# A list scheduler orders each engine's queue in the dense stages, barriers inside them go, and the scan constants are built in two halves

## The chip, the cores and the metric

The kernel runs on all 8 cores of one Trainium2 chip; each core works alone on 2048 of the 16384 tokens and nothing is exchanged. The metric is the device time of the slowest core in microseconds, lower is better. Times of several runs are given by their median; the trace is of one profiled execution on its slowest core, core 7.

## The reference

One decoder layer on `x` (4, 4096, 1024), cut to what matters:

```python
hn = rmsnorm(x, norm1); proj = hn @ w_in            # 1024 -> u, v, s, 512 each
o_a = gmlp(u, v)         # gelu, rmsnorm, causal 128x128 mix per head, product
bu = einsum(b_bar, s)    # S5: 32 groups, 64 complex states each
states = scan(a_bar, bu) # x_t = a * x_{t-1} + bu_t along the whole sequence
y = gelu(real(C @ states) + d_skip * s)
gl = y @ w_glu + b_glu;  o_b = gl[:, :512] * sigmoid(gl[:, 512:])
h = x + concat(rmsnorm(o_a), rmsnorm(o_b)) @ w_out
h = h + hier_moe(rmsnorm(h))      # top-1 of 4 groups, top-2 of 8 experts
h = h + sigmoid(rmsnorm(h) @ w_ple_gate) * (p @ w_ple_proj)
out = rmsnorm(h)
```

A core that holds the second half of a sequence needs the scan's state at its start. It gets it by running the scan's input part over the 2048 tokens before its own (`xprev`, the halo input); cores with a first half do the same work on zeros.

## The kernel before

A small recorder class `Prog` collects every instruction with its engine and its dependencies, and `emit` writes them out: each engine gets its instructions **in the order in which the program text recorded them**, with a semaphore wait where a dependency crosses engines, and also within an engine except on TensorE. `barrier()` (line 176) makes every engine wait for the last instruction of all engines and all open DMAs. `pipeline(nt, stages)` records a loop over tiles in software-pipelined order, the latest stage of the oldest tile first.

The stages, by their place in the text:

- **Setup** (lines 459 to 633): loads of small parameters and of `Wins`, then a chain of VectorE operations on [128, 16] that computes the discretised scan constants, their powers (`pwr`, `Rr`, `Ri`), the big products `PNr/PNi`, `QNr/QNi`, `QMr/QMi` of 2048 columns by `cmul` (six operations each), the copies masked by `hmask` into `QTp` and `QMp`, then on TensorE the matrices `MT` and `PT`. A barrier ends it.
- **A**, the S5 half, in four blocks of 1024 tokens, 0 and 1 from `xprev`, 2 and 3 from `x`. `A_front` loads 8 tiles, normalises (ACT square and copy, rstd on POOL by `rstd_from_ss`), transposes on TensorE, multiplies by `Wins` and transposes again into `Ub2[blk % 2]`. `A_level1` makes the scan input on TensorE into PSUM `psA`/`psB` and scans it on VectorE: 2 halves of 2 segments per block, each segment 4 multiplies out of PSUM, 2 adds, 16 scans, 6 small operations and, for blocks 2 and 3, four more large products of which POOL does two. `A_out(blk, 0)` multiplies by `QTp` and `MT` and applies gelu; `A_out(blk, 1)` transposes, runs the GLU as an 8-step pipeline and transposes into `mixTb`. Order in the text: front 0, front 1, level1 0, front 2, level1 1, front 3, level1 2, level1 3 first half, out(2,0), level1 3 second half, out(2,1), out(3,0), out(3,1). A barrier (line 833) ends it, and only then are the weights `Winu`, `Winv`, `Wout` and the inputs of B loaded.
- **B** (to line 947), the gMLP half and the output projection, 16 tiles of 128 tokens in a pipeline of 10 stages, its result `hd` stored to DRAM. In every second tile POOL issues the load of one expert's weights into the ring (`wload`, 7 of them). A barrier.
- **N** (to line 1016), norm and router logits, 16 tiles, 3 more `wload`; a barrier. **Routing**, one chain of VectorE operations, to the barrier in line 1122.
- **Experts** (to line 1293), gathers, three products and scatters for 32 experts. **C**, the last stage, 16 tiles in a pipeline of 8 stages, to line 1375.

## Time and profile before

| | us |
|---|---|
| median of 3 runs (1679.38 to 1686.72) | 1685.34 |
| the profiled execution, own time | 1668.8 |
| its span, core 7 | 1667.2 |
| spans of the eight cores | 1645.4 to 1667.2 |
| PE busy | 796.6 (48%) |
| DVE (VectorE) busy | 777.6 (47%) |
| ACT (ScalarE) busy | 577.4 (35%) |
| POOL (GpSimd) busy | 375.5 (23%) |

No engine is busy for half of the span. The page's 40 slices show that this is not even over time: DVE leads alone in the first slices and again from 380 to 500 us, PE in stage B. So the reading goes stage by stage, with the busy times of each stretch between two barriers.

### The profile page before, as it was taken

What the parts mean: (1) busy time and instruction counts of PE and PEld (TensorE: products, weight loads), DVE (VectorE), ACT (ScalarE), POOL (GpSimd) and SP (SyncE); (2) the same over time, 40 slices, a digit from 0 to 9 for tenths busy, and PEclk for the clock granted to TensorE, in tenths of its full rate; (3) what the DMA queues carried; (4) which work ended last, traced back from release to release, by engine and by line L of the source; (5) the groups of instructions that cost most, each with busy time, mean ns of one, the idle gap of its engine ahead of it and who ended that gap; (6) DMA issues with size and microseconds to landing.
All of it is one profiled execution on the core that took longest, in us unless ns stands there. A gap on an engine that the chain in (4) does not pass through costs nothing.

```text
span 1667.2 us, 20718 instructions; the slowest of 8 cores (1645.4 to 1667.2 us)
## 1 busy us (share of the span) xinstructions
PE 796.6 (48%) x5539; PEld 509.2 (31%) x5539; DVE 777.6 (47%) x1454; ACT 577.4 (35%) x831; POOL 375.5 (23%) x500
## 2 busy tenths in 40 slices
PE   0041553450244505777644525667555655807663
PEld 0040332330223202333213414455434443503231
DVE  5960226638874403444315673444233432325773
ACT  0004536540025543322204501554324443314543
POOL 0001101102322111322101105333223242202433
PEclk9995775775567856988875557887777877757887
DMA  2005313100000047566568502895557689165651
GB/s 42 0 0 138 90 53 99 63 15 0 1 1 1 0 83 156 159 183 165 151 181 209 165 7 100 301 297 204 181 204 269 224 273 248 45 212 174 235 197 76
DMA packets 68985, 216.76 MB, mean 130 GB/s; under 512 B 16585, under 2 KB 23753, under 8 KB 60368
## 3 DMA queue, kind: packets, MB, share of 16 engines
q1 hardware_dynamic: 42688, 164.97, 29.1%
q0 software_dynamic: 26128, 49.86, 13.4%
q8 instruction: 66, 1.08, 0.3%
q14 instruction: 103, 0.84, 0.2%
HBM read 212.14 MB, written 58.72 MB: 162 GB/s over the span
## 4 chain that ended last, share of the span: by engine, by line
PE 32%; DMA 21%; DVE 17%; issue 15%; ACT 8%; POOL 4%; SPq 1%; DVEq 1%; POOLq 1%; ACTq 0%; PEldq 0%
PE p L360 26%; DVE t L327 8%; DMA yd<-t,t 7%; ACT t L351 5%; PE p L364 5%; DVE t L337 5%; DMA t<-xnd,t 4%; DMA t<-x 3%; POOL t L327 3%; DMA t<-hd 3%; ACT t L355 2%; DVE t L357 2%; DMA t<-w_pg 2%; DVE t L333 1%; DMA t<-xprev 1%
## 5 line engine op out<-in xcount | busy, mean ns | idle before, releaser
L360 PE MATMUL p<-t,t 128*128 128x512 bf16 (+7 forms) x3811 | 636.0, 337 | 322.9 <-DVE t L333 140.5
L360 PEld LDWEIGHTS p<-t,t 128*128 128x128 bf16 (+2 forms) x3811 | 369.7, 121 | 556.2 <-issue 425.1
L364 PE MATMUL p<-t,t 128*128 128x128 bf16 (+1 forms) x1728 | 177.7, 270 | 526.6 <-DVE t L337 185.8
L364 PEld LDWEIGHTS p<-t,t 128*128 128x128 bf16 (+1 forms) x1728 | 142.6, 122 | 580.3 <-issue 575.5
L351 ACT ACTIVATE t<-t 128x1024 bf16<-128x1024 f32 (+4 forms) x172 | 150.8, 878 | 323.5 <-DVE t L327 133.6
L327 DVE TENSOR_TENSOR t<-t,p 128x512 f32<-128x512 f32 (+2 forms) x148 | 105.5, 742 | 330.3 <-PE p L360 258.2
L327 DVE TENSOR_TENSOR t<-t,t 128x512 f32<-128x512 f32 (+10 forms) x343 | 180.2, 547 | 96.7 <-DMA t<-maskS 43.1
L337 DVE SCALAR_TENSOR_TENSOR t<-t,t,t 128x1024 f32<-128x1024 f32 (+2 forms) x144 | 169.2, 1190 | 86.0 <-POOL t L327 61.2
L327 POOL TENSOR_TENSOR t<-t,t 128x1 f32<-128x1 f32 (+3 forms) x184 | 170.0, 928 | 153.6 <-DVE t L327 131.8
L357 DVE COPY t<-p 128x1024 bf16<-128x1024 bf16 (+1 forms) x182 | 122.3, 687 | 166.7 <-DMA yd<-t,t 92.6
L355 ACT COPY t<-p 128x512 f32<-128x512 f32 (+3 forms) x162 | 141.3, 911 | 163.9 <-DMA yd<-t,t 99.9
L333 POOL TENSOR_SCALAR t<-t 128x1 f32<-128x1 f32 x144 | 30.1, 209 | 633.3 <-ACT t L351 599.6
L390 POOL DMA_INDIRECT yd<-t,t x72 | 76.7, 1065 | 201.1 <-DVE t L357 77.2
L355 ACT CAST t<-t 128x1024 bf16<-128x1024 f32 (+2 forms) x100 | 91.8, 930 | 85.4 <-DVE t L337 64.1
L351 ACT ACT_TABLE_LOAD x17 | 21.8, 1283 | 259.2 <-DVE t L327 158.5
L384 POOL DMA_INDIRECT t<-xnd,t x72 | 75.4, 1048 | 62.6 <-DMA t<-xnd,t 35.8
L351 ACT ACTIVATE t<-p 128x512 f32<-128x512 f32 (+1 forms) x100 | 56.9, 590 | 51.4 <-PE p L360 48.8
L327 DVE TENSOR_TENSOR t<-p,t 128x512 f32<-128x512 f32 (+2 forms) x89 | 51.0, 595 | 46.6 <-PE p L360 37.7
L368 DVE TENSOR_TENSOR_SCAN t<-t,t,t 128x64 f32<-128x64 f32 x256 | 63.9, 325 | 0.6 <-DVE t L368 0.6
L357 DVE CAST t<-t 128x1024 bf16<-128x1024 f32 (+3 forms) x77 | 47.8, 625 | 28.7 <-DMA t<-wall 16.2
L355 ACT CAST t<-p 128x512 bf16<-128x512 f32 x28 | 16.0, 587 | 116.2 <-PE p L364 78.8
L351 ACT ACTIVATE t<-t,t 128x1024 bf16<-128x1024 f32 x32 | 36.8, 1150 | 39.6 <-POOL t L327 39.6
(33 smaller groups left out, 181.0 us busy)
## 6 DMA issues: line engine op xcount, KB each, us to landing
t<-wall SPq DMA_DIRECT2D x66, 1024.0 KB, 8.7
t<-x SPq DMA_DIRECT2D x48, 512.0 KB, 4.4
t<-hd SPq DMA_DIRECT2D x32, 512.0 KB, 5.7
t<-yd SPq DMA_DIRECT2D x32, 512.0 KB, 5.7
t<-wall POOLq DMA_DIRECT2D x10, 1536.0 KB, 12.7
t<-xprev SPq DMA_DIRECT2D x16, 512.0 KB, 3.6
hd<-t SPq DMA_DIRECT2D x16, 512.0 KB, 3.2
out<-t SPq DMA_DIRECT2D x16, 512.0 KB, 3.0
```

Of the source, the lines that this page charges most:

```text
L327: self.add(eng, lambda e: e.tensor_tensor(out=out.ap, in0=a.ap, in1=b.ap, op=op), **self._rw(out, (a, b), pw))
L333: self.add(eng, lambda e: e.tensor_scalar(out=out.ap, in0=a.ap, scalar1=self._a(s1), scalar2=self._a(s2), op0=op0, **kw), **self._rw(out, ...
L337: self.add("dve", lambda e: e.scalar_tensor_tensor(out=out.ap, in0=a.ap, scalar=self._a(s), in1=b.ap, op0=op0, op1=op1), **self._rw(out, ( ...
L351: self.add("act", lambda e: e.activation(out=out.ap, in_=a.ap, func=func, **kw), **rw)
L355: self.add("act", lambda e: e.copy(out=out.ap, in_=a.ap), **self._rw(out, (a,), pw))
L357: self.add(eng, lambda e: e.tensor_copy(out=out.ap, in_=a.ap), **self._rw(out, (a,), pw))
L360: self.add("pe", lambda e: e.matmul(out.ap, lhsT=lhsT.ap, rhs=rhs.ap, start=start, stop=stop), reads=list(lhsT.keys) + list(rhs.keys), pwr ...
L364: self.add("pe", lambda e: e.transpose(out=out.ap, in_=a.ap, identity=ident.ap), reads=list(a.keys) + list(ident.keys), pwrites=list(out.k ...
L368: self.add("dve", lambda e: e.tensor_tensor_scan(out=out.ap, data0=d0.ap, data1=d1.ap, initial=self._a(init), op0=ALU.mult, op1=ALU.add), ...
L384: self.add("pool", lambda e: e.indirect_dma_start(out=out.ap, out_offset=None, in_=table.ap, in_offset=bass.IndirectOffsetOnAxis(ap=idx.ap ...
L390: self.add("pool", lambda e: e.indirect_dma_start(out=table.ap, out_offset=bass.IndirectOffsetOnAxis(ap=idx.ap, axis=0), in_=a.ap, in_offs ...
```

## The change

- Every instruction gets an estimated cost and every SBUF and PSUM tile its address range. A tile that is put over older ones takes over their instructions as predecessors (`claim`), so memory is handed on without a barrier.
- The barriers in lines 632, 633, 833, 947 and 1016 are dropped. Those in front of the experts, behind them and at the end stay. They cut the program into segments 0 (setup, A, B, N, routing), 1 (experts) and 2 (C).
- `arrange` orders segments 0 and 2: it goes through the instructions in modelled time and gives each engine, whenever it is free, the ready instruction with the longest remaining chain. A group of accumulating matmuls stays together. The engines still run their queues strictly in that order. The expert stage keeps its order.
- Scratch tiles of the setup are put behind the tiles of the front (`Ub2`, `Zb2`, `xT_blk`, `xst`, `xnb`), so that a front can run beside the setup. `T1`, `T2`, `TA`, `Xr2`, `Xi2` and others of A lie over that scratch.
- The constants are built in two halves of 8 group pairs. The mask goes: `QT` holds both groups of a pair in the two halves of the partitions, and the matmuls read 64 partitions. ACT writes `QT`, and the minus sign of `QM` is made in `cmul`.
- `d_skip` and the B-half gain get their own tile `dg_bc`, the gains of the norms one tile per stage at the same address. The one-hot tiles of the routing have four buffers for two.

```diff
+    def claim(self, key, lo, hi):
+        t = len(self.tiles)
+        inherit = set()
+        for old in self.tiles:
+            if old["lo"] < hi and lo < old["hi"]:
+                inherit |= old["ops"]
+                old["live"] = False
+        self.tiles.append({"lo": lo, "hi": hi, "ops": set(), "inherit": inherit, "live": True, "key": key})
+        assert key not in KEYT, key
+        KEYT[key] = t
+        return t
...
+            if k in KEYT:
+                s["war"] = list(self.tiles[KEYT[k]]["inherit"])
...
+        for k in tuple(reads) + tuple(writes) + tuple(pwrites):
+            if k in KEYT:
+                tl = self.tiles[KEYT[k]]
+                assert tl["live"], k
+                tl["ops"].add(op.idx)
...
+    def arrange(self, ops):
+
+        own = {op.idx: op for op in ops}
+        units = {}
+        for op in ops:
+            units.setdefault((op.eng, op.grp), []).append(op)
+        uid = {}
+        ulist = []
+        for u in units.values():
+            for op in u:
+                uid[op.idx] = len(ulist)
+            ulist.append(u)
+        nu = len(ulist)
+        preds = [set() for _ in range(nu)]
+        succs = [set() for _ in range(nu)]
+        for op in ops:
+            for d in op.deps:
+                if d in own and uid[d] != uid[op.idx]:
+                    preds[uid[op.idx]].add(uid[d])
+                    succs[uid[d]].add(uid[op.idx])
+        cost = [sum(op.cost for op in u) for u in ulist]
+        eng = [u[0].eng for u in ulist]
+        dma = [u[0].is_dma for u in ulist]
+        full = [cost[i] + (2000 + ulist[i][0].size // 250 if dma[i] else 0) for i in range(nu)]
+        order = sorted(range(nu), key=lambda i: ulist[i][0].idx)
+        tail = [0] * nu
+        left = [len(x) for x in succs]
+        stack = [i for i in range(nu) if left[i] == 0]
+        while stack:
+            i = stack.pop()
+            tail[i] = full[i] + max([tail[j] + (60 if eng[j] == eng[i] else 180) for j in succs[i]], default=0)
+            for p in preds[i]:
+                left[p] -= 1
+                if left[p] == 0:
+                    stack.append(p)
+        wait = [len(x) for x in preds]
+        est = [0] * nu
+        avail = {}
+        for i in order:
+            if wait[i] == 0:
+                avail.setdefault(eng[i], []).append(i)
+        free = {}
+        dma_free = 0
+        out = []
+        done = 0
+        while done < nu:
+            best = None
+            for e, lst in avail.items():
+                if not lst:
+                    continue
+                f = free.get(e, 0)
+                t = max(f, min(est[i] for i in lst))
+                if best is None or t < best[0]:
+                    best = (t, e)
+            t, e = best
+            lst = avail[e]
+            pick = max((i for i in lst if est[i] <= t + 40), key=lambda i: (tail[i], -ulist[i][0].idx))
+            lst.remove(pick)
+            start = max(t, est[pick])
+            free[e] = start + cost[pick]
+            end = free[e]
+            if dma[pick]:
+                sz = ulist[pick][0].size
+                b = max(end, dma_free)
+                dma_free = b + sz // 300
+                end = dma_free + 2000
+            out.append((start, done, pick))
+            done += 1
+            for j in succs[pick]:
+                lag = 0 if eng[j] == "pe" and e == "pe" else (60 if eng[j] == e and not dma[pick] else 180)
+                est[j] = max(est[j], end + lag)
+                wait[j] -= 1
+                if wait[j] == 0:
+                    avail.setdefault(eng[j], []).append(j)
+        streams = {}
+        for _, _, i in out:
+            streams.setdefault(eng[i], []).extend(ulist[i])
+        return streams
...
+        for seg in range(self.seg + 1):
+            part = [op for op in ops if op.seg == seg]
+            got = {e: [op for op in part if op.eng == e] for e in engs}
+            if seg in self.sched:
+                head = [op for op in part if op.fn is None]
+                got = self.arrange([op for op in part if op.fn is not None])
+                for e in engs:
+                    got[e] = got.get(e, []) + [op for op in head if op.eng == e]
+            for e in engs:
+                streams[e].extend(got[e])
...
+    def _c(eng, n, k):
+        if eng == "dve":
+            return int(65 + max(110, k * n))
+        if eng == "act":
+            return int(210 + 0.83 * n)
+        return int(150 + 2.0 * n) if n > 1 else 450
...
+        self.add(q, lambda e: e.dma_start(out=oap, in_=iap, **kw), reads=rd, is_dma=True, cls=cls, size=size, cost=(1000 if q == "pool" else 400), **which)
...
+                 reads=list(lhsT.keys) + list(rhs.keys), pwrites=list(out.keys), grp=self.mmg, cost=30 + int(0.42 * _n(rhs)))
...
+    P.sched = {0, 2}
...
-    es_a = Mem(HLO, TOP - 16384)
+    es_a = Mem(HEND, TOP - 16384)
...
-    QTp = P.tile([128, 32, 2, 128], BF16, "QTp", es=es_a)
+    QT = P.tile([128, 16, 2, 128], BF16, "QT", es=es_a)
...
+    Ub2 = [P.tile([128, 32, 128], BF16, f"Ub{i}", es=es_a) for i in range(2)]
+    Zb2 = [P.tile([128, 32, 8, 16], BF16, f"Zb{i}", es=es_a) for i in range(2)]
+    xT_blk = P.tile([128, 8, 1024], BF16, "xTblk", es=es_a)
+    xst = [P.tile([128, 1024], F32, f"xst{i}", es=es_a) for i in range(2)]
+    xnb = [P.tile([128, 1024], BF16, f"xnb{i}", es=es_a) for i in range(4)]
+    sq_scr = P.tile([128, 1024], BF16, "sq_scr", es=es_a)
+    sst = [P.tile([128, 1], F32, f"ss{i}", es=es_a) for i in range(2)]
+    stmp = [P.tile([128, 1], F32, f"stmp{i}", es=es_a) for i in range(2)]
+    srs = [P.tile([128, 1], F32, f"srs{i}", es=es_a) for i in range(2)]
...
-    ctmp = [sm([128, 2048]) for _ in range(4)]
+    ctmp = [sm([128, 1024]) for _ in range(4)]
...
-    S4 = (128, 16, 8, 16)
-    PNr = newt(S4); PNi = newt(S4)
-    cmul(PNr, PNi, rvr.us(3).bc(S4), rvi.us(3).bc(S4), Bbr.us(2).bc(S4), Bbi.us(2).bc(S4), S4)
-    QNr = newt(S4); QNi = newt(S4)
-    cmul(QNr, QNi, pwr.us(3).bc(S4), pwi.us(3).bc(S4), cre.us(2).bc(S4), cim.us(2).bc(S4), S4)
-    QMr = newt(S4); QMi = newt(S4)
-    cmul(QMr, QMi, QNr, QNi, ivr.us(2).us(3).bc(S4), ivi.us(2).us(3).bc(S4), S4)
-    QMp = newt((128, 32, 2, 128))
-    QTv = QTp.re("p (gp h) r c -> p gp h r c", h=2)
-    QMv = QMp.re("p (gp h) r c -> p gp h r c", h=2)
-    for h in range(2):
-        hm = hmask[:, h:h + 1]
-        P.ts(QTv[:, :, h, 0, :], QNr.re("p g j c -> p g (j c)"), hm, ALU.mult, pw=True)
-        P.ts(QTv[:, :, h, 1, :], QNi.re("p g j c -> p g (j c)"), hm, ALU.mult, s2=-1.0, op1=ALU.mult, pw=True)
-        P.ts(QMv[:, :, h, 0, :], QMr.re("p g j c -> p g (j c)"), hm, ALU.mult, pw=True)
-        P.ts(QMv[:, :, h, 1, :], QMi.re("p g j c -> p g (j c)"), hm, ALU.mult, s2=-1.0, op1=ALU.mult, pw=True)
-    with ExitStack() as es_sp:
-        ps_m = [P.ptile([128, 4, 128], F32, f"ps_m{i}", es=es_sp) for i in range(2)]
-        ps_t = [P.ptile([128, 4, 128], F32, f"ps_t{i}", es=es_sp) for i in range(2)]
-        for q4 in range(8):
+    S4 = (128, 8, 8, 16)
+    PN = [newt(S4) for _ in range(2)]
+    QN = [newt(S4) for _ in range(2)]
+    QM = [newt(S4) for _ in range(2)]
+    es_sp = ExitStack()
+    ps_m = [P.ptile([128, 4, 128], F32, f"ps_m{i}", es=es_sp) for i in range(2)]
+    ps_t = [P.ptile([128, 4, 128], F32, f"ps_t{i}", es=es_sp) for i in range(2)]
+    for part in range(2):
+        gs = slice(part * 8, part * 8 + 8)
+        cmul(PN[0], PN[1], rvr[:, gs].us(3).bc(S4), rvi[:, gs].us(3).bc(S4), Bbr[:, gs].us(2).bc(S4), Bbi[:, gs].us(2).bc(S4), S4)
+        cmul(QN[0], QN[1], pwr[:, gs].us(3).bc(S4), pwi[:, gs].us(3).bc(S4), cre[:, gs].us(2).bc(S4), cim[:, gs].us(2).bc(S4), S4)
+        cmul(QM[0], QM[1], QN[0], QN[1], ivr[:, gs].us(2).us(3).bc(S4), ivi[:, gs].us(2).us(3).bc(S4), S4, neg=True)
+        P.cp(QT[:, gs, 0, :], QN[0].re("p g j c -> p g (j c)"), eng="act", pw=True)
+        P.actf(QT[:, gs, 1, :], QN[1].re("p g j c -> p g (j c)"), AF.Copy, scale=-1.0, pw=True)
+        for q4 in range(4):
             pm = ps_m[q4 % 2]
             for k_ in range(4):
-                g = q4 * 4 + k_
-                gp = g // 2
-                P.mm(pm[:, k_, :], PNr[:, gp].re("p i c -> p (i c)"), QMp[:, g, 0, :], True, False)
-                P.mm(pm[:, k_, :], PNi[:, gp].re("p i c -> p (i c)"), QMp[:, g, 1, :], False, True)
-            P.tt(MT[:, q4 * 4:(q4 + 1) * 4, :], pm, maskM.us(1).bc((128, 4, 128)), ALU.mult, pw=True)
-        for q2 in range(8):
+                gp = q4 // 2 * 4 + k_
+                hp = slice(64 * (q4 % 2), 64 * (q4 % 2) + 64)
+                for ri in range(2):
+                    P.mm(pm[:, k_, :], PN[ri][hp, gp].re("p i c -> p (i c)"), QM[ri][hp, gp].re("p j c -> p (j c)"), ri == 0, ri == 1)
+            p0 = part * 8 + q4 // 2 * 4
+            P.tt(MT.re("p (q h) c -> p h q c", h=2)[:, q4 % 2, p0:p0 + 4, :], pm, maskM.us(1).bc((128, 4, 128)), ALU.mult, pw=True)
+        for q2 in range(4):
             pt_ = ps_t[q2 % 2]
             for k_ in range(2):
-                gp = q2 * 2 + k_
-                for ri, pn in ((0, PNr), (1, PNi)):
-                    P.tr(pt_[:, 2 * k_ + ri, :], pn[:, gp].re("p i c -> p (i c)"), ident)
-            P.cp(PT[:, q2 * 2:(q2 + 1) * 2].re("p a b c -> p (a b) c"), pt_, eng="act", pw=True)
-        P.barrier()
-    P.barrier()
+                for ri in range(2):
+                    P.tr(pt_[:, 2 * k_ + ri, :], PN[ri][:, q2 * 2 + k_].re("p i c -> p (i c)"), ident)
+            gp0 = part * 8 + q2 * 2
+            P.cp(PT[:, gp0:gp0 + 2].re("p a b c -> p (a b) c"), pt_, eng="act", pw=True)
+    es_sp.close()
...
-                    o = pY(gl // 4)[:, (gl % 4) * 128:(gl % 4 + 1) * 128]
-                    P.mm(o, Xr[:, gp, 0:NCH], QTp[:, g, 0, :], True, False)
-                    P.mm(o, Xi[:, gp, 0:NCH], QTp[:, g, 1, :], False, False)
+                    o = pY(gl % 2)[:, (gl // 2) * 128:(gl // 2 + 1) * 128]
+                    hp = slice(64 * (g % 2), 64 * (g % 2) + 64)
+                    P.mm(o, Xr[hp, gp, 0:NCH], QT[hp, gp, 0, :], True, False)
+                    P.mm(o, Xi[hp, gp, 0:NCH], QT[hp, gp, 1, :], False, False)
                     P.mm(o, ub[:, g, :], MT[:, g, :], False, True)
                 P.tt(ds_, zb[:, ct * 8:(ct + 1) * 8], dsk_bc[:, ct * 128:(ct + 1) * 128].re("p (g c) -> p g c", g=8).us(2).bc((128, 8, 8, 16)), ALU.mult, eng="pool")
...
     A_out(3, 1)
-    P.barrier()
     es_ps.close()
     load_gain(0)
...
     pipeline(16, [b_s0, b_s1, b_s1b, b_s2, b_s3, b_s4, b_s5, b_s6, b_s6b, b_s7])
-    P.barrier()
     es_ps.close()
...
     pipeline(16, [n_sg, lambda t: None, n_s0, n_s1, n_s2, n_s2b, n_s3])
-    P.barrier()
     es_ps.close()
```

## Rows read from the trace of the kernel before

**Rows 1.** Busy time by stretch, core 7: bounds, engines' busy us (instructions), clock, DMA share, GB/s.
```profile
0.00:52.00 52.00, 0.00 (x0) 0.00 (x0) 29.94 (x183) 3.00 (x4) 1.33 (x5) 1.00 0.22 34
52.00:94.00 42.00, 0.00 (x0) 0.00 (x0) 41.90 (x23) 0.00 (x0) 0.00 (x0) 1.00 0.00 0
...
104.00:127.00 23.00, 20.93 (x160) 19.89 (x160) 5.64 (x10) 4.30 (x8) 0.00 (x0) 1.00 0.00 1
127.00:251.00 124.00, 52.26 (x352) 34.85 (x352) 25.65 (x49) 54.82 (x76) 14.20 (x37) 0.67 0.37 97
251.00:363.00 112.00, 55.30 (x384) 37.37 (x384) 61.50 (x212) 63.62 (x94) 12.72 (x28) 0.65 0.21 62
363.00:491.00 128.00, 28.72 (x306) 21.11 (x304) 102.89 (x271) 13.56 (x14) 32.73 (x20) 0.57 0.00 1
491.00:608.00 117.00, 48.31 (x304) 27.71 (x304) 47.91 (x72) 69.72 (x67) 20.69 (x36) 0.72 0.00 0
608.00:643.00 35.00, 1.87 (x17) 1.66 (x18) 4.39 (x4) 2.71 (x5) 4.19 (x7) 0.50 1.04 195
643.00:862.00 219.00, 156.72 (x818) 70.96 (x815) 87.61 (x109) 62.20 (x141) 50.59 (x99) 0.86 0.61 161
862.00:960.00 98.00, 42.18 (x584) 36.21 (x584) 50.61 (x62) 47.41 (x63) 14.11 (x35) 0.51 0.67 189
960.00:1010.00 50.00, 14.55 (x124) 12.83 (x123) 35.72 (x112) 3.07 (x5) 0.27 (x2) 0.60 0.01 4
1010.00:1462.00 452.00, 273.30 (x2016) 199.18 (x2016) 162.96 (x249) 174.18 (x211) 161.13 (x150) 0.78 0.65 216
1462.00:1500.00 38.00, 3.17 (x23) 2.40 (x24) 9.61 (x8) 5.35 (x9) 2.97 (x6) 0.50 0.68 228
1500.00:1667.20 167.20, 99.32 (x459) 44.97 (x457) 101.33 (x89) 73.49 (x136) 60.62 (x76) 0.81 0.49 171
```

**Rows 2.** Groups by line and shape, 0 to 128 us: the setup's large operations; busy us, mean ns.
```profile
L327 DVE TENSOR_TENSOR t<-t,t 128x2048 f32<-128x2048 f32 x18 | 39.7, 2281 | 0.0
...
L327 DVE TENSOR_TENSOR t<-p,t 128x512 bf16<-128x512 f32 x8 | 5.5, 691 | 12.1 <-PE p L360 11.0 <-PE p L364 1.1
...
L333 DVE TENSOR_SCALAR t<-t,t 128x2048 f32<-128x2048 f32 x4 | 4.9, 1275 | 0.0
```

**Rows 3.** The same view, VectorE, 127 to 251 us: what the halo fronts put on it.
```profile
L357 DVE CAST t<-p 128x512 bf16<-128x512 f32 x12 | 8.3, 692 | 25.5 <-PE p L360 25.5
L333 DVE TENSOR_SCALAR t<-p,t 128x512 bf16<-128x512 bf16 x16 | 7.7, 484 | 68.7 <-PE p L364 63.8 <-ACT t L351 4.7
L357 DVE COPY t<-p 128x1024 bf16<-128x1024 bf16 x6 | 4.0, 687 | 3.7 <-PE p L364 3.7
```

**Rows 4.** Timeline of VectorE (start, length): two halo segments' starts, then two main ones'.
```profile
254.01 2.48 DVE L327 TENSOR_TENSOR t<-t,p 128x512 f32<-128x512 f32 x4
...
262.71 2.48 DVE L327 TENSOR_TENSOR t<-t,p 128x512 f32<-128x512 f32 x4
...
382.53 2.47 DVE L327 TENSOR_TENSOR t<-t,p 128x512 f32<-128x512 f32 x4
...
396.39 2.47 DVE L327 TENSOR_TENSOR t<-t,p 128x512 f32<-128x512 f32 x4
```

**Rows 5.** Groups by shape, ACT, 500 to 608 us: copies of the transposes.
```profile
L355 ACT COPY t<-p 128x1024 bf16<-128x1024 bf16 x12 | 40.5, 3642 | 9.7 <-PE p L364 9.7
```

**Rows 6.** Waits, 611 to 850 us: engine and line, what for, us in total, times, longest.
```profile
ACT t L351 <- DMA t<-x: 72.9, 13, 26.8
```

**Rows 7.** DMA issues of the whole span: queue, count, KB each, median us to landing.
```profile
t<-wall POOLq DMA_DIRECT2D x10, 1536.0 KB, 12.7
...
t<-w_out POOLq DMA_DIRECT2D x1, 2048.0 KB, 42.6
```

**Rows 8.** Groups by shape, POOL: the rstd power, 127 to 251, then 650 to 840 us.
```profile
L327 POOL TENSOR_TENSOR t<-t,t 128x1 f32<-128x1 f32 x18 | 9.9, 549 | 2.7
...
L327 POOL TENSOR_TENSOR t<-t,t 128x1 f32<-128x1 f32 x45 | 35.7, 792 | 8.1 <-POOL t L333 4.2 <-DVE t L357 0.6
```

193 lines of the change are left out of this document (119 added, 74 removed).

## The prediction

> **What bounds the kernel now.** I read the two summaries of the page first (busy time by engine, 40 slices), then cut the span at the barriers [rows 1]. The reader is to see in each stretch which engine is nearly full, and whether another stretch, independent of it, leaves that engine empty. To 94 us only VectorE works: 29.9 us of 52 in a chain of small operations, then 41.9 of 42. From 104 to 127 TensorE builds the matrices and VectorE has 5.6 us. In the halo fronts, 127 to 251 us, VectorE is busy for 25.7 of 124 us; no engine reaches half. From 363 to 491 VectorE is the bound, 102.9 of 128. From 491 to 608 nothing is: VectorE 47.9, ACT 69.7, PE 48.3 of 117. From 608 to 643 the DMA engines are at 1.04 and the others idle: the weights and inputs of B are loaded behind a barrier. In B, PE is busy for 156.7 of 219 us. N has 50.6 of 98 on VectorE, routing is one chain, the experts take 452 us and C 205.2. The A part is thus a row of pieces of work for VectorE with holes between them, and B, N and C are pipelines in which a full turn is longer than any engine's work.
>
> **Setup, halo and scan, to the end of the last scan segment (491 us now).** The fronts of blocks 0 and 1 read nothing of the setup, and their tiles no longer lie on its scratch. So they go beside the 94 us in which ACT, PE and DMA are idle. But `T1`, `T2` and `TA` now lie over the products' temporaries `ctmp`, and `xin_i` over `PN[1]`. The first segment therefore waits for all products of both halves and the last read of `PN[1]`, not for the first half alone. What counts is VectorE's sum:
> - the chain, 52 us [rows 1]. The loads at its start can only come a little earlier.
> - the products: 18 of 2281 ns [rows 2] become 36 of half the width. By this row each costs 1.14 us, and somewhat more for what doesn't halve: 36 x 1.2 = 43 us.
> - the mask: eight multiplies of 1.275 us go, 10.2 us [rows 2]. Four ACT copies take their place, on an idle engine. Eight results of `MT` stay, 5.5 us.
> - eight halo segments, 8.7 us each, and eight main ones, 13.9 us each [rows 4]: 70 + 111 = 181 us. They stay one chain, since `T1`, `T2` and the carried state are one tile each. The waits for POOL within a main segment are in its 13.9.
> - the halo fronts' part, 8.3 + 7.7 + 4.0 = 20 us [rows 3], and the eight results of out(2,0) that stand before the last two segments on `psA`, 8 x 0.69 = 5.5 us by the size of the same results in [rows 2].
>
> Together 307 us. With 4% for queue waits I take 320, between 300 (the chain's waits filled) and 380 (half of the 124 us of the two fronts stays bare). That is **171 us less**. ACT has 54.8 and 63.6 us in the two pairs of fronts and PE 52.3 and 55.3 [rows 1], so both fit in 320 us beside VectorE. If this cover were gone, fronts 0 and 1 would cost their 124 us again. Late next is `A_level1` itself.
>
> **From there to the end of A (117 us now).** out(2,1), out(3,0) and out(3,1) share `y_bf` and follow each other. The transposed copies take 40.5 us of ACT in 12 [rows 5]. They stay, and those of out(3,1) have nothing of A to go beside. Only the inside of the GLU turn and the copies of out(2,1) can move: 105 us, **12 less**; ends 90 and 125.
>
> **The gap (35 us now).** `Winu` and `Winv` lie on `xT_blk` and the x buffers, free after the last front. They load long before use. The `x` tiles of B can come too, from the end of out(3,0). `Wout` has to wait for `Wglu`, and is needed about two tiles later. The seven `wload` are now issued by POOL as soon as their piece of the ring is free. Six of them come at the end of out(3,0). At 12.7 us each [rows 7] that is 76 us of transfer in the 61 us before and some after A's end, and `Wout` (42.6 us beside others [rows 7]) queues behind. I leave 8 us: **27 less**; ends 0 and 45.
>
> **B, N, routing, C.** B turns in 219/16 = 13.7 us with 9.8 us of PE [rows 1]. ACT waits 72.9 us for `x` tiles [rows 6], whose load stands behind the store of `hd` in SP's queue. An order by readiness takes some of that. I take 190 us, **29 less**, between 167 (157 of PE plus filling) and 219. N: 98 us with 50.6 on VectorE and 47.4 on ACT. Its first tiles no longer wait for a barrier, but their buffers lie on B's. I take 80, **18 less**, ends 62 and 98. Routing is a chain, 2 less. The experts keep their order: 452 us. C: 205.2 us with 111 of VectorE and 102.5 of PE, of which 38 are filling. The gain vectors stand before the first `hd` and `yd` loads now; the list puts them later. I take 175, **30 less**, ends 150 and 205. Of what the SP queue is moved past, only the DMA slots (a load waits for the twelfth before it) could bite. All loads of a stage have passed such a slot before.
>
> **Sum.** 171 + 12 + 27 + 29 + 18 + 2 + 30 = 289 us. The span of 1667.2 becomes 1378, the execution's 1668.8 becomes 1380. The median of the runs shown stands 1.0% above that execution (1685.34/1668.8 = 1.0099), so the forecast is 1380 x 1.0099 = **1394 us**.
>
> **A row against the change.** The power of rstd took 549 ns on POOL while VectorE had little to do, and 792 ns on average in B [rows 8]. The fronts' 32 norms now run beside a full VectorE. At B's price that is 32 x 0.24 = 8 us of latency on POOL, which has 14.2 and 12.7 us of work in the fronts [rows 1], and it hides behind VectorE's sum. The sum goes by this. The Trainium skill (SBUF — State Buffer, the section on the doors) says that VectorE and GpSimd share a port pair as an exclusive lock, and that a VectorE operation with two SBUF inputs holds off a GpSimd one that reads SBUF for its whole length. The trace agrees in direction; the size is a rival below.
>
> **The rivals.**
> - *Packed to the bound.* Every stage reaches its lower end: 191 + 27 + 35 + 52 + 36 + 2 + 55 = 398 us less, 1271, by the median's ratio **1283 us**. For it: no stretch but 52 to 94 us has a full engine. Against: single buffers (`y_bf`, `psA`, `psV`, `psD`) and PE at 0.50 to 0.86 of its clock.
> - *Queues stand on wrong prices.* The order is fixed from modelled costs and then obeyed. The copies into `mixTb` are priced at 1.06 us, and ACT's 12 copies took 3.64 us each [rows 5]. A matmul is priced at full clock, and the clock was 0.50 to 0.86. VectorE then stands before a front's copy that comes late, with a scan behind it. Half of the gain goes, 145 us: 1524, or **1539 us**.
> - *The loads in one burst.* `Wout` behind six `wload`: stage B starts 40 us later, **1434 us**.
> - *The overlap isn't there.* Some tile of a front inherits from the setup, and the fronts stay behind it: 80 us come back, **1475 us**. I found no such tile.
> - *Norms held off.* If each of the two POOL operations of a norm waits for one product (1.2 us, above), the 16 norms of the halo fronts take 16 x 2.4 = 38 us longer, and the end moves if the scan then waits for the fronts: 1394 + 38 = **1432 us**. For it: 792 against 549 ns [rows 8]. Against: in that row B's norms lost 0.24 us, not 1.2. This is what the page's lock would do here.
> - *Slower than before.* A load issued just in time for a landing of 2 us plus size, while it takes far longer under load, stands at the head of SP's queue or of its consumer's. Its place is each of the 48 tiles of B, N and C. Against the 289 us it decides from 6.0 us per tile. At 7 us it gives 336 us back, 1394 + 336 x 1.01 = **1733 us**. For it: ACT lost 72.9 us to such loads in 13 waits of B already [rows 6], 5.6 us each. Against: buffers are as deep as before, and the order can only issue a load earlier or at the same place.
>
> **How the numbers follow.** Forecast 0.50, packed 0.15, wrong prices 0.19, burst 0.06, no overlap 0.04, norms held off 0.03, slower 0.03. The range leaves out the far halves of packed and of wrong prices and the slower case: 1290 to 1525 us. Half a per cent is about what a measurement of this kernel can tell from no change. Faster by more 0.95, within it 0.02 (wrong prices at double size), slower 0.03.
>
> **What would show it.** In the trace of after: transposes on PE and squares on ACT before 50 us, and VectorE without a hole from there; the last scan near 320 us (300 to 380); the first `Winu` matmul near 430; all seven `wload` issued before it; a turn of B near 11 us and of C near 8; the experts 452 us long, about 1200 in. Wrong prices would show as idle time of VectorE put down to PE or ACT in the middle of the setup's products. The prediction is wrong if the scan isn't VectorE's sum but waits for the fronts.

## The result and the profile after

The changed kernel takes 1397.07 us (median of 4 runs, 1392.64 to 1399.64); the kernel before, run beside it, takes 1686.03 us (4 runs, 1679.38 to 1703.48). The ratio is 0.827 with a 95% interval of 0.8205 to 0.8336. The forecast was 1394 us, between 1290 and 1525. The total is right by luck: one stage is 60 us late, and others make it good.

| | forecast, us | after, us | before, us |
|---|---|---|---|
| to the end of the scan stage | 320 | 380 | 491 |
| rest of A | 105 | 83 | 117 |
| gap before B | 8 | 6 | 35 |
| B | 190 | 157 | 219 |
| N | 80 | 82 | 98 |
| routing | 48 | 48 | 50 |
| experts | 452 | 460 | 452 |
| C | 175 | 183 | 205 |

The profiled execution took 1399.6 us, its span is 1398.1 us on core 3; the eight spans are 1372.3 to 1398.1 us (before: 1645.4 to 1667.2). These are the stretches of after that answer to [rows 1], routing (707 to 755) left out. Columns as there:

```profile
0.00:52.00 52.00, 2.20 (x9) 1.48 (x9) 38.99 (x191) 15.03 (x22) 6.35 (x17) 1.00 0.47 107
52.00:105.00 53.00, 29.89 (x152) 27.83 (x152) 38.12 (x43) 8.04 (x11) 0.00 (x0) 0.82 0.06 20
105.00:156.00 51.00, 29.36 (x218) 20.19 (x218) 13.84 (x24) 26.13 (x37) 6.76 (x17) 0.72 0.40 104
156.00:380.00 224.00, 126.66 (x884) 75.42 (x882) 204.96 (x537) 104.68 (x156) 64.18 (x77) 0.70 0.25 59
380.00:468.00 88.00, 44.05 (x253) 23.23 (x252) 29.48 (x44) 58.24 (x44) 19.18 (x27) 0.60 0.90 151
468.00:625.00 157.00, 133.69 (x824) 66.27 (x824) 92.42 (x115) 65.99 (x143) 48.96 (x97) 0.92 0.68 171
625.00:650.00 25.00, 0.00 (x0) 0.00 (x0) 0.07 (x2) 0.60 (x1) 0.00 (x0) 0.50 1.02 206
650.00:707.00 57.00, 34.74 (x594) 30.91 (x594) 49.13 (x62) 47.49 (x64) 26.36 (x32) 0.65 0.66 199
...
755.00:1215.00 460.00, 272.02 (x2016) 196.68 (x2016) 162.29 (x247) 173.43 (x210) 163.58 (x151) 0.79 0.66 213
1215.00:1398.10 183.10, 94.64 (x480) 43.04 (x480) 122.48 (x96) 79.24 (x145) 95.55 (x81) 0.77 0.61 202
```

Three stretches say where to look. From 105 to 156 us no engine is full: that is a halo front standing bare, with no other work beside it. From 625 to 650 us nothing computes and the DMA share is 1.02. In B the clock is 0.92, against 0.86 before [rows 1].

**The bare front.** This is the timeline of TensorE from the start (start, length, form, idle time before and its releaser):

```profile
49.36 2.22 PE L531 MATMUL p<-t,t 128*128 128x128 f32 x8 [49.36 <-DVE t L491]
51.97 1.94 PE L531 MATMUL p<-t,t 128*128 128x128 f32 x8 [0.40 <-ACT t L519]
64.87 11.93 PE L527 MATMUL p<-t,t 64*128 64x128 f32 x64 [10.96 <-DVE t L491]
...
92.67 11.93 PE L527 MATMUL p<-t,t 64*128 64x128 f32 x64 [10.20 <-DVE t L491]
105.55 1.87 PE L531 MATMUL p<-t,t 128*128 128x128 bf16 x16 [0.95 <-DVE t L491]
```

Until 104.6 us TensorE works for the setup only (f32). The first transposes of `A_front(0)` (bf16) start at 105.55 us, when the last read of the setup's PSUM tile is over. Squares and norms of six tiles did run early (ACT has 15 us in the first 52), then the front stood. The first scan starts at 160.66 us. In the code, `ps_m` and `ps_t` take PSUM banks 0 to 3, and `psN` and `psZ` of the fronts take the same four; by `claim` they inherit the setup's operations.

**The hole before N.** The first lines are the timelines of POOL's and SP's issues, the last is ACT's first work in N (idle before, releaser):

```profile
605.19 0.81 POOL L551 DMA_DIRECT2D t<-wall  x1 [0.18 <-PE p L527]
619.25 1.61 POOL L551 DMA_DIRECT2D t<-wall  x2 [6.53 <-PE p L527]
```

```profile
620.55 11.14 SPq L551 DMA_DIRECT2D hd<-t  x2
642.09 2.07 SPq L551 DMA_DIRECT2D t<-hd  x4
```

```profile
649.40 1.06 ACT L515 ACTIVATE t<-t 128x1024 bf16<-128x1024 f32 x1 [34.61 <-DMA t<-hd]
```

The list issues the three remaining expert loads (1536 KB each) between 605 and 621 us, as soon as their pieces of the ring are free. The last stores of `hd` and N's first loads of it come into the same queues of the DMA engines. VectorE's last addition of B waits 9.1 us for its `x` tile and ends at 625.0 us; N's first square starts at 649.4.

### The profile page after: what moved, and what is told of

It is laid out like the page before. It is cut to its first block, busy times and chain, and to the rows that moved or that the text cites. A ratio compares the mean times of both kernels' runs of the same rounds, so it can differ in the third digit from the quotient of the medians.

```text
span 1398.1 us, 20754 instructions; the slowest of 8 cores (1372.3 to 1398.1 us)
## 1 busy us (share of the span) xinstructions
PE 781.1 (56%) x5539; PEld 497.7 (36%) x5539; DVE 786.5 (56%) x1464; ACT 581.3 (42%) x835; POOL 431.2 (31%) x500
## 4 chain that ended last, share of the span: by engine, by line
PE 34%; DMA 21%; issue 16%; DVE 15%; ACT 7%; POOL 4%; SPq 1%; DVEq 1%; POOLq 1%; ACTq 0%; PEldq 0%
PE p L527 28%; DMA yd<-t,t 8%; DVE t L491 8%; PE p L531 6%; ACT t L515 4%; DMA t<-xnd,t 4%; DVE t L501 3%; DVE t L521 3%; ACT t L519 2%; DMA hd<-t 2%; DMA t<-w_pg 2%; POOL t L491 2%; DMA t<-x 1%; DMA t<-xprev 1%; DVE t L535 1%
## 5 line engine op out<-in xcount | busy, mean ns | idle before, releaser
L527 PE MATMUL p<-t,t 128*128 128x512 bf16 (+8 forms) x3811 | 630.6, 330 | 167.5 <-DVE t L491 102.7
L527 PEld LDWEIGHTS p<-t,t 128*128 128x128 bf16 (+4 forms) x3811 | 363.6, 121 | 402.5 <-issue 239.0
L531 PE MATMUL p<-t,t 128*128 128x128 bf16 (+1 forms) x1728 | 172.7, 263 | 429.6 <-DVEq L436 98.3
L531 PEld LDWEIGHTS p<-t,t 128*128 128x128 bf16 (+1 forms) x1728 | 138.5, 119 | 477.0 <-issue 468.4
L501 DVE SCALAR_TENSOR_TENSOR t<-t,t,t 128x1024 f32<-128x1024 f32 (+2 forms) x144 | 180.5, 1275 | 136.8 <-POOL t L491 105.2
L491 POOL TENSOR_TENSOR t<-t,t 128x1 f32<-128x1 f32 (+3 forms) x184 | 198.7, 1082 | 113.8 <-DVE t L491 52.7
L515 ACT ACTIVATE t<-t 128x1024 bf16<-128x1024 f32 (+3 forms) x174 | 153.2, 883 | 178.4 <-DVE t L491 46.1
L491 DVE TENSOR_TENSOR t<-t,t 128x8 f32<-128x8 f32 (+10 forms) x359 | 186.4, 550 | 12.2 <-ACT t L515 1.8
L497 POOL TENSOR_SCALAR t<-t 128x1 f32<-128x1 f32 x144 | 55.6, 386 | 385.2 <-ACT t L515 381.0
L535 DVE TENSOR_TENSOR_SCAN t<-t,t,t 128x64 f32<-128x64 f32 x256 | 68.6, 339 | 0.3
L515 ACT ACTIVATE t<-p,t 128x512 bf16<-128x512 bf16 x48 | 30.0, 684 | 33.2 <-PE p L531 32.8
## 6 DMA issues: line engine op xcount, KB each, us to landing
t<-wall POOLq DMA_DIRECT2D x10, 1536.0 KB, 23.4
```

The source lines that it names most:

```text
L491: self.add(eng, lambda e: e.tensor_tensor(out=out.ap, in0=a.ap, in1=b.ap, op=op), cost=self._c(eng, _n(out), 1.14), **self._rw(out, (a, b) ...
L497: self.add(eng, lambda e: e.tensor_scalar(out=out.ap, in0=a.ap, scalar1=self._a(s1), scalar2=self._a(s2), op0=op0, **kw), cost=self._c(eng ...
L501: self.add("dve", lambda e: e.scalar_tensor_tensor(out=out.ap, in0=a.ap, scalar=self._a(s), in1=b.ap, op0=op0, op1=op1), cost=self._c("dve ...
L515: self.add("act", lambda e: e.activation(out=out.ap, in_=a.ap, func=func, **kw), cost=self._c("act", _n(out), 1) + (190 if accum is not No ...
L527: self.add("pe", lambda e: e.matmul(out.ap, lhsT=lhsT.ap, rhs=rhs.ap, start=start, stop=stop), reads=list(lhsT.keys) + list(rhs.keys), pwr ...
L531: self.add("pe", lambda e: e.transpose(out=out.ap, in_=a.ap, identity=ident.ap), reads=list(a.keys) + list(ident.keys), pwrites=list(out.k ...
```

## The experiments

All are edits of the changed kernel, called "after" here; ratios are to the kernel before, run on the same chip. After's own time is from another chip, so a difference of two medians in us also holds what sets two chips apart. A gain "by the ratios" is the difference of two ratios times 1680 us; it is good to some 12 to 15 us. Where the traces tell more closely, they are used.

### Order and barriers

**x2_text**: the change with all queues in the order of the text. What remains of it are the dropped barriers, the memory hand-over, and the constants in halves without the mask.

```diff
-    P.sched = {0, 2}
+    P.sched = set()
```

> The kernel after, but every queue in the order of the program text in all stages; the barriers stay away, memory is handed on by tile, the constants are built in halves. Theory (the order is what pays): only the load gap of 35 us, some 10 us of the mask and a few us at each former barrier are gained, about 1620 us. Rival (dropping the barriers pays most, the order little): 1500 us or less.

Measured: 1638.85 us, ratio 0.9783 (0.9696 to 0.987). The scan's last segment starts its scans at 469.5 us (480.6 before). So only 2 of the 17 per cent (1.3 to 3.0) come without the new order.

**x3_barr**: the new order, but with barriers again after A, B and N; the setup's barriers stay out (the segments are numbered anew by it).

```diff
-    P.sched = {0, 2}
+    P.sched = {0, 1, 2, 3, 5}
...
     A_out(3, 1)
+    P.barrier()
...
     pipeline(16, [b_s0, b_s1, b_s1b, b_s2, b_s3, b_s4, b_s5, b_s6, b_s6b, b_s7])
+    P.barrier()
...
     pipeline(16, [n_sg, lambda t: None, n_s0, n_s1, n_s2, n_s2b, n_s3])
+    P.barrier()
```

> The kernel after with barriers again between A and B, B and N, N and routing; each part is still ordered by the list. Theory (handing memory on without a barrier pays 27 to 30 us at A to B and some at B to N): 45 us more than after, 1442 us. Rival (the load burst that replaces the gap costs as much as the gap did): within 10 us of after, and stage B's first tiles turn in under 10 us for the 12 us of after.

Measured: 1470.59 us, ratio 0.8779 (0.8696 to 0.8861), 73.5 us slower than after by the medians, where 45 were expected. From A's last copy to B's last addition it takes 238 us (455.2 to 693.3), after takes 162 (462.8 to 625.0). This is the stretch behind the barrier at A's end, and TensorE's timeline there:

```profile
455.00:510.00 55.00, 11.29 (x43) 4.92 (x44) 5.09 (x5) 5.30 (x9) 9.49 (x14) 0.57 1.01 190
```

```profile
506.03 5.24 PE L527 MATMUL p<-t,t 128*128 128x512 bf16 x16 [24.77 <-DMA t<-w_in]
```

The first products of B start at 473.6 us but the second half of `Winu`/`Winv` lands only at 506, since all the loads held by the barrier go out at once. The gap that the change removes was a burst at a barrier, as the prediction had read it [rows 1, 7]. What that barrier cost in the kernel before isn't shown by the 76 us, though: here all seven expert loads go into the burst (458 to 465 us), where the kernel before spreads them over B.

**x6_ctext**: C alone in the order of the text (`P.sched = {0}`).

> The kernel after, but stage C keeps the order of the program text; only segment 0 is ordered by the list. Theory (the order of C is worth the difference seen in the traces): C is about 22 us longer, 1419 us, and its turn goes back to 9.6 us. Rival (C is shorter in after only because of other things, as the loads' order after the barrier): 6 to 10 us.

Measured: 1415.18 us, ratio 0.843 (0.8399 to 0.8461), against 0.827: 18 us slower by the medians, 27 by the ratios. From C's first load to the end it is 193.9 us there (from 1222.55), 173.5 in after (from 1224.68) and 194.4 in the kernel before (from 1472.81). So in C the order is worth 20 us, as expected, and nothing else in the change shortened it. What the run shows about the engines stands in the last section.

### The scan stage

**x1_psum**: a pad of four banks in front of the setup's PSUM tiles puts them into banks 4 to 7, which only the scan's `psA` and `psB` use later. Nothing else changes.

```diff
     es_sp = ExitStack()
+    P.ptile([128, 4, 512], F32, "ps_pad", es=es_sp)
     ps_m = [P.ptile([128, 4, 128], F32, f"ps_m{i}", es=es_sp) for i in range(2)]
```

> The kernel after with one edit: the setup's PSUM tiles ps_m and ps_t lie in banks 4 to 7 instead of 0 to 3. In the changed kernel the halo fronts' transposes into psN (banks 0 and 1) inherit from ps_m, and the first of them ran at 105.6 us, the first scan segment at 156.7 us. Theory (PSUM hand-over holds the fronts): the first transpose runs before 30 us, the first scan segment starts at about 110 us, and the time falls by about 45 us to 1352 us. Rival (the fronts' copies, put between the products on VectorE, delay the constants): first segment near 130 us, 20 us less. Rival (the fronts wait for the constants through another tile): no change.

Measured: 1360.19 us (1357.32 to 1361.71), ratio 0.8123 (0.8069 to 0.8177): 37 us faster than after by the medians, 25 by the ratios. TensorE's timeline, the groups by shape inside its last line (16 small ones left out), and two stretches (to the first scan, and on to the end of the scans):

```profile
10.67 0.59 PE L531 MATMUL p<-t,t 128*128 128x128 bf16 x4 [10.67 <-ACT t L515]
...
91.39 11.93 PE L527 MATMUL p<-t,t 64*128 64x128 f32 x64 [9.70 <-DVE t L491]
...
119.98 22.00 PE L527 MATMUL p<-t,t 64*128 64x128 f32 x120 [0.79 <-DVE t L491]
```

```profile
L527 PE MATMUL p<-t,t 128*128 128x512 bf16 x40 | 11.7, 456 | 0.0
L527 PE MATMUL p<-t,t 64*128 64x128 f32 x64 | 10.0, 352 | 0.8 <-DVE t L491 0.8
```

```profile
52.00:141.00 89.00, 63.84 (x389) 47.86 (x390) 69.45 (x98) 40.15 (x58) 12.96 (x25) 0.75 0.25 78
141.00:342.00 201.00, 115.81 (x798) 67.74 (x796) 193.63 (x517) 87.22 (x129) 55.35 (x62) 0.66 0.21 48
```

The transposes of front 0 start at 10.67 us instead of 105.55. The last scan is at 339.1 us; it is at 371.6 in after and between 365.4 and 369.9 in x3_barr, x4_pace and x9_route, which don't touch this stage. The bare front was the PSUM hand-over; this is shown, since the edit moves nothing but the banks. But only 26 to 33 of the 60 us come back. That is less than the 45 of the theory and nearer the first rival: the first scan is still at 141.0 us. The reason can be read from the setup, which now ends 37 us later than in after (142.0 for 104.6). These are a parameter's load and VectorE's first large product, in x1_psum, then in after:

```profile
t<-are SPq DMA_DIRECT2D x1, 8.0 KB, 12.2
66.04 1.22 DVE L491 TENSOR_TENSOR t<-t,t 128x1024 f32<-128x1024 f32 x1
...
t<-are SPq DMA_DIRECT2D x1, 8.0 KB, 3.1
43.45 13.71 DVE L491 TENSOR_TENSOR t<-t,t 128x1024 f32<-128x1024 f32 x12
```

The list now issues the front's first `xprev` tiles ahead of the small parameter loads, which land in 12.2 instead of 3.1 us; the fronts' copies stand between VectorE's operations; and 40 products of a front stand among the last 64 `MT` products. The large products start 23 us later, the last `MT` products 27 us later (119.98 for 92.67), and with the front's among them they last 10 us longer. From 141 us on, VectorE is busy for 193.6 of 201 us: there the stage does run at VectorE's sum.

**x5_k128**: the `y` products of `A_out` over all 128 partitions.

```diff
-                    P.mm(o, Xr[hp, gp, 0:NCH], QT[hp, gp, 0, :], True, False)
-                    P.mm(o, Xi[hp, gp, 0:NCH], QT[hp, gp, 1, :], False, False)
+                    P.mm(o, Xr[:, gp, 0:NCH], QT[:, gp, 0, :], True, False)
+                    P.mm(o, Xi[:, gp, 0:NCH], QT[:, gp, 1, :], False, False)
```

> The kernel after, but the y matmuls of A_out read all 128 partitions of Xr, Xi and QT instead of 64. Its part left out: the two groups of a pair are no longer kept apart, so y holds the sum of both. In after the y matmuls of 64 partitions took 184 ns each, in the kernel before the masked ones of 128 partitions 77 ns. Theory (half the partitions cost time on PE, also on the path of out(3,0)): PE busy falls by about 13 us in all and the time by 8 to 12 us to 1387 us. Rival (it was only the clock, 0.50 for 0.74, and the ACT copies bound this stretch): the mean of one stays at 150 ns or more, time within 3 us.

It leaves out that the two groups of a pair are kept apart. Measured: 1394.28 us (1387.28 to 1404.85), ratio 0.8321 (0.827 to 0.8371): no difference from after. To 480 us TensorE has 20.1 us for the 192 bf16 products of 128x128 in this line, where after has 43.8. The products did get shorter, as the theory said, but they are off the path.

**x12_k128**: x1_psum, with the `MT` products over all 128 partitions.

```diff
-                    P.mm(pm[:, k_, :], PN[ri][hp, gp].re("p i c -> p (i c)"), QM[ri][hp, gp].re("p j c -> p (j c)"), ri == 0, ri == 1)
+                    P.mm(pm[:, k_, :], PN[ri][:, gp].re("p i c -> p (i c)"), QM[ri][:, gp].re("p j c -> p (j c)"), ri == 0, ri == 1)
```

> As x1_psum, but the f32 matmuls for MT read 128 partitions instead of 64. Its part left out: MT sums both groups of a pair. In after 64 of them took 11.93 us at a granted clock of 1.00, 186 ns each; in the kernel before 128 took 16.7 us, 131 ns each, also at 1.00. Theory (half the partitions cost PE time, the products wait for it): 131 ns each again, the first scan segment 5 us earlier than in x1_psum, the time 0 to 5 us less. Rival (the operand layout makes them slow): 186 ns again.

It leaves out the same separation in `MT`. Measured: 1359.67 us in 2 runs, ratio 0.8098 (0.8024 to 0.8172): no difference from x1_psum. The first scan is at 136.6 us (141.0). The first 64 products took 10.12 us at a granted clock of 0.72, against 11.93 at 0.50 in x1_psum. Neither 186 nor 131 ns came out, but 158.

**x7_price**: the copies into `mixTb` are priced at 4600 ns, as measured, instead of the model's 1.06 us.

```diff
-            P.cp(dst, pq.re("p (j c) -> p j c", j=8), eng="act", pw=True)
+            P.cp(dst, pq.re("p (j c) -> p j c", j=8), eng="act", pw=True, cost=4600)
```

> The kernel after, but the scheduler prices the eight copies into mixTb at 4600 ns, which they took in the trace of before, instead of 1060 ns. Theory (wrong prices cost: ACT's gelu and squares stand behind these copies): A's end comes 5 to 10 us earlier, 1390 us. Rival (the order changes little where the chain has nothing else to do): within 3 us of after.

Measured: 1385.31 us (1381.45 to 1394.73), ratio 0.826 (0.8217 to 0.8304) beside 0.827. The median is 12 us lower, but by the ratios there is no difference, and A's last copy ends at 456.3 us, where it ends at 456.7 in x5_k128, run beside it with the old price. This one price, wrong by a factor of four, costs next to nothing. The general rival of wrong prices isn't excluded by it, but its best candidate is.

### The loads of the experts' weights

**x9_route**: the last three expert loads go behind N, beside the routing, in which the DMA share was 0.01 [rows 1]. (`wload` hands the operation in its second argument to the DMA as one more to wait for; so too in x4 and x11.)

```diff
-        if t % 4 == 2 and NBB + t // 4 < NB:
-            wload(NBB + t // 4)
...
     pipeline(16, [n_sg, lambda t: None, n_s0, n_s1, n_s2, n_s2b, n_s3])
+    for k_ in range(NBB, NB):
+        wload(k_, [P.last["dve"]])
```

> The kernel after, but the last three expert weight loads (7 to 9) wait for N's last VectorE operation, so that they run in the routing, where the DMA share was 0.00. In after two of them and the third left at 619 us, the last hd stores took 11 us to issue and nothing ran from 625 to 649 us at a DMA share of 1.02. Theory (these loads hold the last x and hd transfers): the hole falls from 25 to about 8 us, the time by 15 to 20 us to 1380 us; the experts don't wait, since weights 7 to 9 are needed late. Rival (as pacing showed, the bytes of loads 0 to 6 are what fills the queues): no change within 5 us.

Measured: 1369.07 us (1364.99 to 1369.8), ratio 0.8152 (0.8128 to 0.8176): 28 us faster than after by the medians, 20 by the ratios. POOL's issue and ACT's first work in N:

```profile
683.53 2.36 POOL L551 DMA_DIRECT2D t<-wall  x3 [0.58 <-DVE t L491]
```

```profile
622.30 1.06 ACT L515 ACTIVATE t<-t 128x1024 bf16<-128x1024 f32 x1 [12.07 <-DMA t<-hd]
```

N's first square is at 622.3 instead of 649.4 us, and the experts' loads start at 728.3 instead of 755.3. Some 6 of these 27 us stand already at the last scan (365.4 for 371.6), which the edit doesn't touch. The hole itself, from B's last addition to N's first square, falls from 24.4 to 6.2 us, and x5_k128 and x7_price, run beside x9 with the loads in their old place, have their experts' loads at 746.6 and 748.3. So the three loads cost 18 to 20 us, the upper end of what was expected. The experts don't miss the weights.

**x4_pace**: each expert load waits for an operation of its own pipeline turn instead of leaving when its memory is free.

```diff
-            wload(t // 2)
+            wload(t // 2, P.last["dve"])
...
-            wload(NBB + t // 4)
+            wload(NBB + t // 4, P.last["act"])
```

> The kernel after, but each expert weight load waits for the VectorE add of its tile in B (or ACT's copy in N), so that they leave one by one as in the kernel before. In after six are issued by 406 us and the last two of N in one burst at 619 us; the first two turns of B took 12 us, and nothing ran from 625 to 649 us. Theory (the burst holds up x, Wout and hd): B's start and the hole before N shrink, 20 to 25 us less, 1374 us. Rival (the same bytes only move): within 5 us of after.

Measured: 1398.98 us (1395.87 to 1403.21), ratio 0.8357 (0.8298 to 0.8415): no gain, as the rival said. A's end is free of expert loads, but two of the seven now go out at 596.6 and 607.7 us, and VectorE and ACT wait at the same place:

```profile
626.24 1.22 DVE L491 TENSOR_TENSOR t<-t,p 128x1024 f32<-128x1024 f32 x1 [8.15 <-DMA hd<-t]
```

```profile
648.88 1.06 ACT L515 ACTIVATE t<-t 128x1024 bf16<-128x1024 f32 x1 [38.12 <-DMA t<-hd]
```

N's first square stands at 648.9, as in after. Pacing moved the transfers to a place where they are as much in the way; x9_route moved them out of it.

**x10_psroute**: x1_psum and x9_route together.

> Both edits that shortened the kernel after: the setup's PSUM in banks 4 to 7 (25 us less by the ratios 0.8123 and 0.827) and the last three expert loads in the routing (20 us less, 0.8152). Theory (they act at two places of the path, the scan's start and the hole before N, and add up): ratio 0.800, about 1345 us beside a before of 1680. Rival (an earlier A moves work into the same full DMA stretch, so the second gain is partly lost): ratio 0.810.

Measured: **1340.87 us** (1340.25 to 1344.91), ratio 0.7994 (0.7955 to 0.8032). By the ratios that is 46 us better than after, where the two alone gave 25 and 20 (by the medians 56, with 37 and 28 alone): they add up, as expected. With x11_psrp, which can't be told from it, it is the fastest kernel of the study. The last scan is at 335.7, the first product of B at 432.5, N's first square at 590.8 us.

**x11_psrp**: x10, and four of the loads in B wait for VectorE's additions.

```diff
-            wload(t // 2)
+            wload(t // 2, [P.last["dve"]] if t >= 6 else ())
```

> As x10_psroute, and expert loads 3 to 6 wait for the VectorE add of tiles 6, 8, 10 and 12 of B, loads 0 to 2 leave as before. In after the two first turns of B took 12 us at a DMA share above 1 and the later ones 8. Theory (the six loads at once hold up the first x tiles and Wout): the first turns fall to 9 us, 5 to 8 us less than x10_psroute. Rival (the bytes only move into the later turns, as with full pacing): no change or up to 10 us more.

Measured: 1344.93 us (1338.57 to 1354.66), ratio 0.8029 (0.7981 to 0.8077): no difference from x10. N's first square comes at 601.2 us, 10 later. Two of the paced loads leave at 557.6 and 573.7 us, so the pace again puts loads in front of N.

## Why the prediction was right, and where it wasn't

**The scan stage: the mechanism of the sum held, its start failed.** The step was "The fronts of blocks 0 and 1 read nothing of the setup, and their tiles no longer lie on its scratch". That is true of SBUF and false of PSUM. The prediction even had the rival, "The overlap isn't there", at 0.04, and wrote "I found no such tile". VectorE's busy time is near the sum: 38.99 + 38.12 + 13.84 + 204.96 = 295.9 us to 380. My 307 hold the chain's 52 us, in which VectorE was busy for 29.9 [rows 1], so they mean 285 busy and, with the 4 per cent, 35 idle; 84 idle were measured, 65 of them before 156 us. So 11 of the 60 us are work and 49 are waiting. The prediction named "waits for the fronts" as its sign of being wrong, and from 105 to 156 us that is what VectorE does: there its mechanism failed, and the total doesn't heal that. x1_psum shows that the hand-over of four PSUM banks is about half of the miss. The other half shows in x1_psum as the late start of the first scan (141 us; the chain's 52, the products' 43 and some 10 for the results and multiplies in front of it, an estimate, give 105). Taking the fronts beside the setup was to cost the setup nothing; in x1_psum the setup ends 37 us later, by the late parameter loads, the fronts' copies on VectorE and their products on TensorE. No run splits these. The width of the `MT` products is little of it: x12_k128 took 4 us away. The rival's price, 80 us, was near: the stage is 60 us late.

**The rest of A (83 us for 105).** The step "Only the inside of the GLU turn and the copies of out(2,1) can move" was too narrow. ACT's timeline shows the strided copies of out(2,1) from 387.6 us and those of out(3,1) from 444.6 to 462.8:

```profile
387.62 13.78 ACT L519 COPY t<-p 128x1024 bf16<-128x1024 bf16 x3 [11.83 <-PE p L531]
...
444.56 18.26 ACT L519 COPY t<-p 128x1024 bf16<-128x1024 bf16 x4 [3.70 <-PE p L531]
```

The GLU of out(2,1) already ran between the last scan segments (TensorE has its products from 345.7 to 368.2 us), so a part of this stage was done under the scan stage's cover. A stage that waits for VectorE leaves TensorE and ACT free for the stage behind it; a sum by stages can't see that. This gave back 22 of the 60 us; the stage lies below its lower end of 90.

**The gap (6 us for 8).** Right. The last copy of A ends at 462.8, the first `Winu` product starts at 468.4. Its mechanism is also right: x3_barr has the hole again. The rival of the burst (`Wout` behind six loads, 40 us) didn't come, but the transfers are slow all the same: the DMA issues list an expert load at 23.4 us to landing, 12.7 before [rows 7]. B's first two turns take 12 us each. Of the signs, all seven `wload` do stand before the first `Winu` product (the last at 434.6 us).

**B (157 us for 190).** The mis-sized term is the floor, "157 of PE plus filling". I took TensorE's busy time for a fixed amount of work. This row is TensorE in the middle of B, the next the 512 large products of B by shape (busy us, mean ns, idle before):

```profile
500.00:600.00 100.00, 98.31 (x654) 50.38 (x653) 72.45 (x90) 50.89 (x114) 38.48 (x77) 1.00 0.70 184
```

```profile
L527 PE MATMUL p<-t,t 128*128 128x512 bf16 x512 | 119.9, 392 | 4.3 <-DVE t L521 2.3 <-DVE t L491 1.1 <-ACT t L519 0.9
```

TensorE is busy for 98% and the granted clock is 1.00. The same 512 products took 140.7 us before, at 0.86. With its holes filled, the engine's own time shrank from 156.7 to 133.7 us. In the middle a turn is some 8 us (51.5 matmuls of a tile, 654 in 100 us), not 11. This is 33 us better than forecast, and below the lower end of 167 that I had given the term.

**N and routing (82 and 48 us for 80 and 48).** The number is right by two errors. N's own work is 57 us, five less than the lower end of 62, and the hole in front of it 25 us. The prediction saw that the expert loads would move ("The seven `wload` are now issued by POOL as soon as their piece of the ring is free") and looked for the harm at A's end. The three behind them did the harm at B's. x9_route shows the cause: with them gone from there, the hole is 6 us.

**The experts (460 for 452).** The list doesn't order this stage, and what the 8 us are wasn't tested. It isn't the core: in both kernels cores 3 and 7 show the stage in the same bounds.

**C (183 for 175).** Within its range of 150 to 205. It is 22 us shorter, and x6_ctext shows that 20 are the order's, not the forecast 30. VectorE and POOL both have more busy time in the new order (below); that this is the missing part would fit and isn't shown. It is the behaviour of the rival "norms held off", which I had only put on the halo fronts. There it was small: POOL's power of rstd took 558 ns to 156 us and 647 from there to 380, against 549 before [rows 8]; in C it took 946.

**Slower than before.** Its mechanism, loads issued too late at the head of a queue, can be read in B: ACT waits for `x` tiles 9.1 us in 4 waits. Before it was 44.8 in 11; the 72.9 in 13 that I laid on B's turns hold 28.1 us in 2 waits of the gap ahead of B, since [rows 6] start at 611 us. Loads left early, not late. **The sum.** +60 - 22 - 2 - 33 + 2 + 0 + 8 + 8 = 21 in rounded stages; the span, 1398, is 20 us above the forecast 1378. The median was to be 1.0% above the profiled execution and is 0.2% below it, which takes back most of that. The total was right because +60 of one stage met -55 of two others, and nothing in the prediction says that they should.

## What to carry to other kernels

When memory is handed on by address, compare the two stages' tiles in PSUM as well as in SBUF before you call them independent: one pad in front of a tile was worth about 25 us. When you lay one chain beside another, ask what the first loses: here the setup lost 37 us to the fronts, and an expected gain of 45 became 25. A greedy list issues a transfer as soon as it may, and what it may harm is the next small load, so look at what is due when the big ones are on the way; here moving three loads out of a transition was worth about 20 us and pacing them nothing. And TensorE's busy time at a granted clock of 0.86 was no floor for a denser schedule: the same 512 products took 15% less in the denser B, at 0.92.
